# Fewer seven-product weight units, and the second group of weight sums made later, in a two-block transformer kernel

## The reference

```python
def sqrelu_mlp(hn, w1, w2):            # w1 1024 x 4096
    u = jnp.square(jax.nn.relu(hn @ w1))
    return u @ w2

def swiglu(h, w_in, w_out):            # w_in 1024 x 5632, used twice (two layers)
    gate, up = jnp.split(h @ w_in, 2, axis=-1)
    return (jax.nn.silu(gate) * up) @ w_out
```

## Time and profile before

| what | us |
|---|---|
| median of three executions | 2040.6 |
| the profiled execution, its own time | 2041.61 |
| span of its instructions | 2039.8 |
| PE busy | 1953.4 |
| DVE busy | 1267.8 |
| ACT busy | 833.1 |
| POOL busy | 310.5 |

### The profile page before, as it was taken

The page is one execution under the profiler, slowest core; times in us unless marked ns, Lnnn a source line. Parts: engine busy times, 40 slices in busy tenths (PEclk is TensorE's granted clock), DMA queues, the critical chain, the costliest instruction groups (busy, mean ns, idle before and its releaser), DMA issues.

```text
span 2039.8 us, 29719 instructions
## 1 busy us (share of the span) xinstructions
PE 1953.4 (96%) x12230; PEld 1719.2 (84%) x12230; DVE 1267.8 (62%) x1769; ACT 833.1 (41%) x1131; POOL 310.5 (15%) x253
## 2 busy tenths in 40 slices
PE   8999989999999999999999999999997899999996
PEld 6788867789898887999899999998884578889894
DVE  6668766656574654121558477576797558667475
ACT  4448734533232334223354143244434445234242
POOL 2122231200110130011320000001245110000002
PEclk9999999999999998998999999999998899999998
DMA  9753141599999658610165334342121023344341
GB/s 336 208 128 133 62 105 65 178 353 237 222 245 351 245 136 185 150 62 22 63 164 187 119 145 147 119 154 103 63 96 50 21 98 130 127 158 150 113 172 62
DMA packets 68480, 299.14 MB, mean 147 GB/s; under 512 B 6505, under 2 KB 6633, under 8 KB 48386
## 3 DMA queue, kind: packets, MB, share of 16 engines
q1 hardware_dynamic: 38064, 201.15, 27.2%
q0 software_dynamic: 30128, 96.08, 19.8%
q10 hardware_dynamic: 162, 0.10, 0.0%
HBM read 295.19 MB, written 94.96 MB: 191 GB/s over the span
## 4 chain that ended last, share of the span: by engine, by line
issue 43%; PE 43%; POOL 4%; DVE 3%; DMA 3%; ACT 3%; SPq 0%; POOLq 0%; DVEq 0%; ACTq 0%
PE lin L582 27%; POOL squares L801 2%; PE lin L1884 2%; PE aux L1884 1%; PE aux L1474 1%; PE aux L2720 1%; DMA w_raw<-weight_sums 1%; DMA w_sum<-weight_sums 1%; ACT w_hi L491 1%; PE lin L1676 1%; DMA w_raw<-in_weights 1%; PE lin L1429 1%; POOL w_lo L498 1%; PE lin L2690 1%; PE aux L2704 1%
## 5 line engine op out<-in xcount | busy, mean ns | idle before, releaser
L582 PE MATMUL lin<-x_hi,w_hi 128*128 128x512 f32 (+1 forms) x1160 | 409.4, 353 | 16.5 <-DVE tmp L677 6.5
L582 PE MATMUL lin<-x_hi,w_lo 128*128 128x512 f32 (+1 forms) x1160 | 407.5, 351 | 0.0
L582 PE MATMUL lin<-x_lo,w_hi 128*128 128x512 f32 (+1 forms) x1160 | 407.1, 351 | 0.0
L498 DVE TENSOR_TENSOR w_lo<-w_raw,w_hi 128x2048 fp32r<-128x2048 f32 (+1 forms) x101 | 228.8, 2265 | 149.1 <-ACT w_hi L491 148.8
L491 ACT ACTIVATE w_hi<-w_raw 128x2048 fp32r<-128x2048 f32 (+1 forms) x112 | 210.3, 1878 | 207.2 <-PE lin L582 193.2
L582 PEld LDWEIGHTS lin<-x_hi,w_hi 128*128 128x128 f32 x1160 | 219.8, 190 | 51.8 <-DVE tmp L677 7.4
L582 PEld LDWEIGHTS lin<-x_lo,w_hi 128*128 128x128 f32 x1160 | 220.1, 190 | 30.2 <-issue 0.2
L582 PEld LDWEIGHTS lin<-x_hi,w_lo 128*128 128x128 f32 x1160 | 219.9, 190 | 29.9
L801 POOL TENSOR_TENSOR squares<-squares,tmp 128x512 f32<-128x512 f32 (+2 forms) x72 | 96.9, 1346 | 972.5 <-ACT tmp L781 969.9
L582 PE MATMUL lin<-v_hi,w_hi 128*128 128x264 f32 (+1 forms) x704 | 237.7, 338 | 6.0 <-DVE tmp L2412 3.5
L582 PE MATMUL lin<-v_hi,w_lo 128*128 128x264 f32 (+1 forms) x704 | 234.1, 333 | 0.0
(11 more groups left out here) (451 smaller groups left out, 4395.1 us busy)
## 6 DMA issues: line engine op xcount, KB each, us to landing
w_raw<-in_weights SPq DMA_DIRECT2D x112, 1024.0 KB, 4.8
w_raw<-in_weights SPq DMA_DIRECT2D x43, 768.0 KB, 6.0
w_sum<-weight_sums SPq DMA_DIRECT2D x43, 768.0 KB, 4.6
weight_sums<-in_weights POOLq DMA_DIRECT2D x4, 5120.0 KB, 50.0
weight_sums<-in_weights POOLq DMA_DIRECT2D x2, 7168.0 KB, 56.5
w_raw<-weight_sums SPq DMA_DIRECT2D x43, 256.0 KB, 6.3
weight_sums<-in_weights POOLq DMA_DIRECT2D x8, 1280.0 KB, 14.3
weight_sums<-weight_sums POOLq DMA_DIRECT2D x8, 1280.0 KB, 13.3
```

Of the source, the lines that this page charges most:

```text
L498: does.tensor_tensor(w_lo[:, s, 0:n], w_raw[:, s, 0:n], w_hi[:, s, 0:n].bitcast(F32), ALU.subtract).then_inc(sem("w_lo_ready"), 1)
L582: last = nc.tensor.matmul(o, a, b, start=(k % (L.kc // k_banks) == 0 and p == 0), stop=((k + 1) % (L.kc // k_banks) == 0 and p == 2))
```

## The change

The table of quad units loses nine: unit 2 in each of ff1b, ff1c, ff1d; unit 5 in up0a and up1a, unit 4 in up0b and up1b, unit 3 in up0c and up1c. These become plain units. The rest of each up part is no longer evenly spaced and is cut in two runs, so that an up group has six runs in place of three. In POOL's program the base, pairs and triples of up1 move from before the gates of GLA to behind the sum of squares for the first SwiGLU norm (l_ffn0), right before the fours.

```diff
--- before.py
+++ after.py
@@ -72,9 +72,9 @@
 ]
 
 
-QUADS = {"ff1b": (1, 2, 3), "ff1c": (1, 2, 3), "ff1d": (1, 2, 3),
+QUADS = {"ff1b": (1, 3), "ff1c": (1, 3), "ff1d": (1, 3),
          **{f"up{n}{part}": at for n in range(2)
-            for part, at in zip("abc", ((3, 4, 5, 6, 7), (1, 2, 3, 4, 5, 6, 7), (1, 2, 3, 4, 5)))}}
+            for part, at in zip("abc", ((3, 4, 6, 7), (1, 2, 3, 5, 6, 7), (1, 2, 4, 5)))}}
 BLOCK_W = 512
 
 
@@ -3028,14 +3028,14 @@
             pool_quad_pairs(pool, "up0")
             pool_quad_triples(pool, "up0")
             pool_quad_fours(pool, "up0")
-            pool_quad_base(pool, "up1", *"abc")
             pool_squares(pool, l_mix0, l_mix0.idx)
-            pool_quad_pairs(pool, "up1")
-            pool_quad_triples(pool, "up1")
             next_splits_after(pool, GR)
             dve_splits(pool, GR, nc.gpsimd)
             pool_gates(pool)
             pool_squares(pool, l_ffn0, l_ffn0.idx)
+            pool_quad_base(pool, "up1", *"abc")
+            pool_quad_pairs(pool, "up1")
+            pool_quad_triples(pool, "up1")
             pool_quad_fours(pool, "up1")
             pool_squares(pool, l_mix1, l_mix1.idx)
```

## The result

The changed kernel takes 2046.99 us (median of 10 executions, 2045.17 to 2055.79), the kernel before 2037.02 us in 10 executions. The ratio is 1.0068, with a 95% interval of 1.0051 to 1.0087: slower by 0.7%. The two medians differ by 10 us, while the ratio stands for 13.9 us; the 35 executions of the changed kernel that the record lists one by one have a median of 2051.77 us, nearer to the ratio. The profiled execution took 2051.53 us with a span of 2049.7 us, 9.9 us more than the span before.

What follows compares the result with a forecast made beforehand. PE was taken to set the pace in the MLPs, except for a load wait in ff1d. Terms 12.2 - 6.1 + 3.0 = +9.1 us on 2041.6 gave 2050.7, said as 2050 on the median; range 2044 to 2058.

Steps and rivals of the forecast that it cites:

- rival 1: At up0a the base of up1 costs nothing: net +6.1 us, 2046.7; chance 0.24.
- nine plain units: In the first MLP, up0 and up1, three each: plain units in place of quad units cost PE 12.2 us.
- ff1d without the base of up1: In ff1d the last two units lose their wait and half clock: -6.1 us, bounds -5 and -6.5.
- the base at up0a: In up0a the base delays unit 4's w_sum load, then unit 5: +3 us, bounds 0 and 10.0.
- rival 3: Borders between quad and plain units cost 1 us each at nine places: +9 on the forecast, 2059; chance 0.07.
- 0.3 us more: In up0a, plain unit 5 ready at 1097.3 against 1097.0 for PE, added to unit 4's delay of 1.4 us.
- 1.4 us at the fourth product: In unit 4 of up0a, the fourth product waits 1.4 us for its bank, held by DVE's late first row.
- The Trainium skill's sentence on turns between queues: At up0a, DMA engines alternate queues by packet: w_sum load about twice 5.3 us, 10.6, under the 10.7 allowed, term 0.
- Rival 2: At up0a w_sum lands after 20.7 us: term 10 and 1.7 for the clock, net +17.8, 2058; chance 0.12.
- Rival 4: In GLA, up1's pairs and triples had slowed the stage: some 15 us return, net -6, 2035; chance 0.07.
- No change: Whole kernel: a time that measurement can't tell from before, within about 0.3% (6.1 us), border 2046.7; chance 0.20.

Runs made afterwards that it cites:

- the third experiment: The changed kernel, with POOL waiting ahead of the base of up1 until dn0a's first weight unit has landed: ratio 1.0041 to the kernel before.
- the first experiment: Nine quad units made plain, POOL's order left as in the kernel before: ratio 1.0046 to the kernel before, median 2050.5 us against 2039.86.
- the second experiment: All 43 quad units kept, POOL's order as in the changed kernel: ratio 1.0068 to the kernel before.
- the fourth experiment: Kernel before, all 43 quad units; up1's base and pairs in the GLA stage, triples and fours behind l_ffn0's squares: ratio 0.9984, median 2037.13 us.

## Why the prediction was right, and where it was not

The forecast was +9.1 us on the profiled execution. The windows give +10.5, and the two spans differ by 9.9. The median of ten, 2046.99 us, would fit rival 1 (2046.7) better than the forecast (2050), but the ten executions of the kernel before have a median of 2037.02 in place of the 2040.6 from which both were reckoned. It is the windows that tell the two apart. That the sum came so near is in part luck: the first term was 0.7 us too high and the last 2.2 us too low.

| step | predicted | measured by windows |
|---|---|---|
| nine plain units | +12.2 | +11.5 |
| ff1d without the base of up1 | -6.1 | -6.2 |
| the base at up0a | +3.0 | +5.2 |
| sum | +9.1 | +10.5 |

**Nine plain units: right.** ff1b took 1.07 us more, ff1c 1.21 (ff1d is counted at 1.21 too), the three parts of up0 1.48 each, those of up1 1.22, 1.18 and 1.18. Where nothing else bears on a stage, that is all there is, so borders between quad and plain units cost nothing (rival 3 falls; the third experiment shows the same for up0a).

**ff1d: the size and the wait were right, the credit was not.** The stage went from 47.10 to 42.15 us, which with 1.21 for the plain unit is -6.2. The prediction said that the wait goes with the base, and in the changed kernel POOL's queue is indeed empty beside ff1d. But it gave the gain to the move of the base out of POOL's order, and the first experiment shows that the smaller table alone gives the same window. The prediction itself noted that up0's sums end earlier with 14 units, but did not follow it to the base behind them, which would have been drawn ahead of ff1d. By the second experiment the move would have done it as well. So the whole change paid 5.2 us at up0a for something that it had already.

**The base at up0a: right in place and kind, mis-sized.** 96.76 - 90.08 - 1.48 = 5.2 us in place of 3.0. The reckoning in the text came to 1.7 and 1.7 for the clock, the value taken was 3. Measured, the parts are: unit 4 took 13.34 us from start to start against 10.19, 3.15 more; unit 5 took 13.21 against 11.67, 1.54 more, which is a clock of 0.88 for 13.2 us; about 0.5 came at the end of the part. The w_sum landed after 10.4 us in place of 11.5, and p6 was not late. The step that failed is the one that came to "0.3 us more" for unit 5. It took a landing at 1090, which is 1086.3 on the changed kernel's scale (measured 1086.8), then 4.1 us of splits and 3.2 us of DVE's steps. Measured from landing to the first matmul are 8.2 us: 0.7 until ACT came to w_hi, since L2370 and L1904 stand ahead of it, 4.2 of splits, 3.2 of DVE's steps, 0.15 to PE. Landing and work together put the start of unit 5 1.4 us later than reckoned, half of it ACT's own row of work ahead of the split, which was left out. The prediction of 1.4 us at the fourth product was wrong as well: there PE lost about 0.2, and the lateness came out whole at the next unit's start instead.

**Rival 1 (nothing at up0a)** fell, though its condition held: the w_sum landed within the 10.7 us that it allowed. The price was not at p6 but behind it, where the DVE steps of unit 3 were 3.8 us late.

The Trainium skill's sentence on turns between queues ("DMA: Bandwidth & Descriptors", Queues, rings and completion order) gave an estimate of 10.6 us for this load. The measured 10.4 us is near it by luck, for the 5.3 us that it doubled was not the time of a load alone. In the kernel before, POOL's fours ran beside that load. From 1074.2 to 1079.5 the row of POOL's queue was:

```profile
q0 software_dynamic: 245, 0.47, 48.8%
```

Alone, in the third experiment, the load took 4.4 us. So the base made it 2.4 times as long, and the 1 MB load behind it too (15.9 us against 6.5). That is more than the twice that even turns would give, and the trace does not agree with the estimate.

**Rival 2 (a landing of 20.7)** fell for this kernel. In the second experiment, where quad units are neighbours all through, the loss was of its size, 16.6 us, but not by its cause. The load of 19.3 us there was that of unit 3, issued at 1037.17, for which nobody waited; the same load took 19.3 us in the changed kernel too. The four that ACT waited for landed after 10.5 to 12.3 us.

**Rival 4 (GLA relieved)** fell: 302.8 us before, 302.0 after, 301.4 with the base put there.

**No change** had a chance of 0.20. The interval begins at 1.0051, outside the 0.3% that the prediction took as its border.

## What to carry to other kernels

A large copy in another queue is paid for where a one-buffer load is issued late and used at once. Put it beside stages that have no such load: here beside GLA, a down-projection or quad units with a plain one between them it was free, beside neighbouring quad units it cost 5 to 17 us. Before a stall is credited to an edit of the order, ask whether another part of the same change already moves the traffic away, by making what is ahead of it in the queue shorter. And when a load comes late, walk the chain through every engine's order to the next unit's start: the first user may be on time and the second not.

## What was not expected of the hardware

**The scatter of one kernel's times follows the granted clock.** The changed kernel took 2045 to 2063 us in 35 executions, with a mean granted clock from 0.983 down to 0.974. Within a kernel the times have a standard deviation of 1.6 to 5.1 us, the times multiplied by the clock one of 1.1 to 3.2 us. On this scale the kernel before stands at 1997.5 and 1997.2 (29 and 23 executions), the changed one at 2007.8, the table alone at 2004.9, the move alone at 2005.9, the base beside dn0a at 2005.0, the kernel without neighbours in up0a at 2005.3, the base in GLA at 1994.7, and the version with the fours beside dn0a at 1992.6. The change is +10.3 us there, near the +10.5 of the windows, while the ratio gives +13.9; the clock is on record to 0.001, which is 2 us, so a single execution says little. The mean clock of the changed kernel was 0.9785, that of the kernel before 0.9794 in its 29 executions and 0.9787 in the other 23, so a lower clock of the changed kernel is not shown. Much of the scatter of the spans has one place: the stretch from dn0c to the first quad unit of up1a took 334.1 to 344.4 us in the eight profiled executions, at a mean clock of 0.97 down to 0.95, though its work is the same in all.

**A short idle time was paid twice.** In up0a PE sat idle for 2.68 us; then unit 5 ran 1.54 us longer than its 11.67, PE busy throughout, at a granted clock of 0.88. In ff1d of the kernel before it was the same pattern with 2.50 us and a clock of 0.89. Behind the 1.37 us of idle time in the fourth experiment dn0a took 46.72 us, against 46.64 before: there nothing followed.

**Two loads of one queue suffered alike from the copy in the other.** The base of 14 units took 58.3 us (14.68 MB, some 250 GB/s). Beside it the 768 KB w_sum load took 10.4 us against 4.4 without it, and the 1 MB load right behind 15.9 against 6.5 (third experiment): 2.4 times each. The median of 4.7 us for a 1 MB load in ff1d would be the wrong measure for the second, since none of those had a w_sum load just ahead of it.
